# A two-layer decoder step: the indexer of layer 0 in one sequence, selection by tile, layer 1's attention steps in another order

## The reference, cut to what matters

```
I[t,s] = sum_h w[t,h] * relu(q_idx[t,h] . k_idx[s]) * 64**-0.5      # 8 heads, 64 wide, one shared key
keep[t] = top 128 (prompt) or 256 (sample) causal keys of I[t]      # ties: lowest index first
A[t]    = softmax over keep[t] of q.k * 64**-0.5, times V           # mixer A; mixer B (stick-breaking) uses all keys
C[t]    = (softmax1 - lambda * softmax2) V                          # layer 1, 8 heads, 4 KV heads
```

## Time and profile before

| | |
|---|---|
| median of 3 runs | 2282.15 us (2279.0 to 2286.1) |
| profiled execution | 2285.52 us, span 2283.7 us |
| busy | TensorE 2009.0, VectorE 742.9, ScalarE 420.9, GpSimd 267.4 us |
| granted TensorE clock | 0.938 of full on average |
| read from HBM | 255.30 MB, 115 GB/s over the span |

### The profile page before, as it was taken

The page is one execution under the profiler, slowest core; times in us unless marked ns, Lnnn a source line. Parts: engine busy times, 40 slices in busy tenths (PEclk is TensorE's granted clock), DMA queues, the critical chain, the costliest instruction groups (busy, mean ns, idle before and its releaser), DMA issues.

```text
span 2283.7 us, 32506 instructions
## 1 busy us (share of the span) xinstructions
PE 2009.0 (88%) x11272; PEld 1443.8 (63%) x11272; DVE 742.9 (33%) x1642; ACT 420.9 (18%) x771; POOL 267.4 (12%) x482
## 2 busy tenths in 40 slices
PE   7889957887768999999998997777788999999996
PEld 5447624544556777777776772344466777777775
DVE  2268975646501421110001421655523311200002
ACT  1120114454502200000001200333333100000000
POOL 3000221221110000000000000232200000000000
PEclk9999977988779999999999998998899999999998
DMA  7101053967641122111211113888701221212111
GB/s 236 41 22 64 0 218 142 338 237 271 231 176 65 56 70 68 64 65 65 73 64 64 48 63 119 283 291 266 263 21 54 69 69 64 73 57 73 64 65 59
DMA packets 95091, 264.45 MB, mean 116 GB/s; under 512 B 13650, under 2 KB 20051, under 8 KB 94355
## 3 DMA queue, kind: packets, MB, share of 16 engines
q0 software_dynamic: 46560, 167.80, 20.9%
q1 hardware_dynamic: 44146, 88.86, 11.5%
q10 hardware_dynamic: 4288, 6.51, 0.8%
HBM read 255.30 MB, written 7.82 MB: 115 GB/s over the span
## 4 chain that ended last, share of the span: by engine, by line
PE 70%; DVE 16%; DVEq 3%; ACT 3%; issue 3%; ACTq 2%; DMA 2%; SPq 1%; PEldq 0%
PE ps L485 53%; DVE arena L1427 4%; PE ps L541 2%; PE ps L842 1%; DVE arena L1308 1%; DVE small L1684 1%; PE ps L907 1%; DMA arena<-in_kv_ab 1%; PE ps L730 1%; PE ps L862 1%; PE ps L706 1%; PE ps L666 1%; DVEq L1312 1%; ACT arena L1219 1%; ACTq L329 1%
## 5 line engine op out<-in xcount | busy, mean ns | idle before, releaser
L485 PE MATMUL ps<-hs,wring 128*128 128x288 f32 x3520 | 872.4, 411 | 24.9 <-ACT hs L993 16.4
L485 PEld LDWEIGHTS ps<-hs,wring 128*128 128x128 f32 x3520 | 675.0, 192 | 220.5 <-issue 20.1
L485 PE MATMUL ps<-arena,wring 128*128 128x288 f32 x2048 | 500.5, 408 | 5.7 <-DVE arena L1342 5.7
L485 PEld LDWEIGHTS ps<-arena,wring 128*128 128x128 f32 x2048 | 391.0, 191 | 115.3 <-issue 6.6
L414 POOL DMA_DIRECT2D wring<-in_weights x170 | 90.2, 530 | 1386.3 <-PE ps L485 1385.0
L1340 DVE TENSOR_TENSOR arena<-arena,norm 128x576 f32 x64 | 48.5, 758 | 371.6 <-ACT arena L1012 365.2
L1297 DVE TENSOR_TENSOR norm<-norm 128x576 f32<-128x576 f32 x24 | 18.2, 759 | 448.6 <-ACT norm L1003 448.6
L1012 ACT ACTIVATE arena<-ps 128x576 f32 (+1 forms) x76 | 49.5, 651 | 527.2 <-PE ps L485 527.2
L1003 ACT ACTIVATE norm<-ps 128x576 f32<-128x576 f32 x32 | 20.8, 651 | 631.7 <-PE ps L485 631.7
L344 POOL DMA_DIRECT2D arena<-in_kv_ab x128 | 68.7, 537 | 278.6 <-PE ps L716 155.7
L344 POOL DMA_DIRECT2D arena<-in_kv_c x128 | 68.7, 537 | 215.6 <-PE ps L907 95.6
(11 more groups left out here) (231 smaller groups left out, 1804.8 us busy)
## 6 DMA issues: line engine op xcount, KB each, us to landing
wring<-in_weights POOLq DMA_DIRECT2D x174, 512.0 KB, 3.7
arena<-in_kv_ab SPq DMA_DIRECT2D x128, 320.0 KB, 5.0
arena<-in_kv_ab POOLq DMA_DIRECT2D x128, 320.0 KB, 6.5
arena<-in_kv_c SPq DMA_DIRECT2D x128, 256.0 KB, 4.0
arena<-in_kv_c POOLq DMA_DIRECT2D x128, 256.0 KB, 4.6
arena<-in_w_v_ab SPq DMA_DIRECT2D x1, 2592.0 KB, 24.6
xs<-in_x_t SPq DMA_DIRECT2D x4, 576.0 KB, 9.3
out_y_t<-xs SPq DMA_DIRECT2D x4, 576.0 KB, 2.8
```

The costliest lines, as they stand in the source:

```text
L485: mm = pe.matmul(out[:, h * 512:h * 512 + TH], wring[:, slot, k], inp[:, b * KD + k, h * TH:(h + 1) * TH], start=(b == 0 and k == 0), stop ...
```

## The change: what it does

**Indexer.** The twelve prompt units and the eight sample batches run in one sequence, `ORDER_I`, on TensorE and ScalarE. All query blocks (`qz8`) and head weights (`wz`, 32 columns for each batch) are staged once ahead of it. The Relu results of all eight batches are kept (`relu8`). The weighted sums come at the end: pair `p` of batches goes to partitions 32p to 32p+31 of `ps[2]` and `ps[3]`, by matmuls with 32 columns of weights. `clear` is gone.

**Rotations of mixer A** move from between the token-major tiles to behind the last five of the 13 projections, into `ps[2]` and `ps[3]`.

**Selection by tile.** After the search only tile 0 (the samples) is turned into a mask ahead of the attention; tiles 1 to 3 are done by `chosen(t)` in steps 1, 2 and 3 of the attention, ahead of `q_max(t)`. A memset and the wait for the store of the indexer keys move ahead of the search.

**Layer 1's steps.** On TensorE `p_turn` goes to the head of the step, `p_sums` runs a step earlier than before (unit n-2), the five `c_turn` are spread as 0 | 1, 2 | 3 | 4 over the quarters, each ahead of its values. On ScalarE `p_turn_out` goes to the head. On VectorE `p_out` goes to the head (unit n-3), `c_out` and one `c_turn_out` ahead of `p_mix`.

The diff, cut to its core:

```diff
+        ROT_A = 8
+        s_i = norm0[:, 0:2048].rearrange("p (r x) -> p r x", r=2)
+        UNITS_I = [(2 * it + r, i) for it in range(2) for r in range(2) for i in range(1, 4)]
+        ORDER_I = "S0 P0 P1 S1 P2 S2 P3 P4 S3 P5 S4 P6 P7 S5 P8 S6 P9 P10 S7 P11".split()
@@ TensorE, indexer
+            def i_sample(b):
+                p, s = b // 2, b % 2
+                if s == 0:
+                    pe.wait_ge(kidx_landed[p], 16 * (PAGES if p < 2 else 2 * PAGES))
+                    if p < 2:
+                        pe.wait_ge(kidx_landed_pool[p], 16 * PAGES)
+                if b:
+                    pe.wait_ge(i_relu, b)
+                q = qz8[s][:, p]
+                for h in range(2):
+                    pe.matmul(ps[2][:, h * 512:(h + 1) * 512], q, kx[s][:, p * 1024 + h * 512:p * 1024 + (h + 1) * 512], start=True, stop=True)
+                pe.matmul(ps[3][:, 0:NS], q, qk[:, IK, SEQ:T], start=True, stop=True).then_inc(i_qk, 1)
...
+            pe.wait_ge(i_staged, 1)
+            for what in ORDER_I:
+                if what[0] == "P":
+                    i_prompt(int(what[1:]))
+                else:
+                    i_sample(int(what[1:]))
+            pe.wait_ge(i_relu, NB)
+            parts = [(ps[2], 0, 0, 512), (ps[2], 512, 512, 512), (ps[3], 0, HALF, NS)]
+            for n, (t, lo, at, w) in enumerate(parts):
                 for s in range(2):
+                    for p in range(NB // 2):
+                        mm = pe.matmul(t[32 * p:32 * p + 32, lo:lo + w], wz[:, 2 * p + s], relu8[2 * p + s][:, at:at + w],
+                                       start=(s == 0), stop=(s == 1))
@@ TensorE, rotations of mixer A behind the projections
+            dense(G_AB + N_I, O_AB + N_I, N_AB - N_I, hs, peel=N_AB - N_I, after=rotate_a)
+            pe.wait_ge(rope_read, 5)
+            token_major(0, wv, 640, 16)
@@ TensorE, layer 1
             for n in range(STEPS_C):
                 b, quarter = n // 4, n % 4
+                if 2 <= n < UNITS_C + 2:
+                    p_turn(n - 2)
                 if n < UNITS_C:
                     p_scores(n)
                 if quarter == 0 and b < NB:
                     c_keys(b, 0)
                     c_keys(b, 1)
+                if quarter == 0 and b:
+                    c_turn(b - 1, 0)
                 if quarter == 1 and b >= 2:
                     c_pick(b - 2)
+                if quarter == 1 and b:
+                    c_turn(b - 1, 1)
                 if quarter == 1 and b < NB:
                     for g in range(2, 5):
                         c_keys(b, g)
                 if quarter == 1 and b:
-                    c_turn(b - 1, 0)
+                    c_turn(b - 1, 2)
                 if quarter == 2 and b:
-                    c_turn(b - 1, 1)
+                    c_turn(b - 1, 3)
                     c_values(b - 1, 0)
-                    c_turn(b - 1, 2)
                     c_values(b - 1, 1)
                 if quarter == 3 and b:
-                    c_turn(b - 1, 3)
+                    c_turn(b - 1, 4)
                     c_values(b - 1, 2)
-                    c_turn(b - 1, 4)
                     c_values(b - 1, 3)
                     c_values(b - 1, 4)
                 if 2 <= n < UNITS_C + 2:
-                    p_turn(n - 2)
-                if 3 <= n < UNITS_C + 3:
-                    p_sums(n - 3)
+                    p_sums(n - 2)
@@ VectorE, selection
+            dve.wait_ge(ik_stored, 16)
+            dve.memset(qz0, 0.0)
...
+            def chosen(j):
+
+                w = SEL_W[j]
+                thr = thr_b[:, j:j + 1]
+                dve.tensor_scalar(out_p[:, 0:w], scores[j], thr, None, ALU.is_gt, ALU.add, accum_out=cnt[:, j:j + 1])
+                dve.tensor_scalar(eq_p[:, 0:w], scores[j], thr, None, ALU.is_equal, ALU.add, accum_out=cnt[:, 0:1])
+                dve.drain()
+                dve.tensor_tensor(rest[:, j:j + 1], C["topk"][:, j:j + 1], cnt[:, j:j + 1], ALU.subtract)
+                dve.tensor_tensor_scan(cum_p[:, 0:w], eq_p[:, 0:w], eq_p[:, 0:w], 0.0, ALU.add, ALU.bypass)
+                dve.drain()
+                dve.scalar_tensor_tensor(eq_p[:, 0:w], cum_p[:, 0:w], rest[:, j:j + 1], eq_p[:, 0:w], ALU.is_le, ALU.mult)
+                dve.drain()
+                dve.tensor_tensor(eq_p[:, 0:w], eq_p[:, 0:w], out_p[:, 0:w], ALU.add)
+                dve.drain()
+                dve.tensor_scalar(scores[j], eq_p[:, 0:w], -1.0, BIG, ALU.add, ALU.mult)
+                dve.drain()
@@ VectorE, layer 0's attention
+                if 1 <= t < 4:
+                    chosen(t)
                 if t < UNITS_A:
                     q_max(t)
@@ VectorE, layer 1
+                if 3 <= n < UNITS_C + 3:
+                    p_out(n - 3)
                 if n < UNITS_C:
                     p_max(n)
+                if quarter == 1 and b >= 2:
+                    c_out(b - 2)
+                if quarter and b:
+                    c_turn_out(b - 1, (1, 3, 4)[quarter - 1])
                 if 1 <= n < UNITS_C + 1:
                     p_mix(n - 1)
...
-                if 4 <= n < UNITS_C + 4:
-                    p_out(n - 4)
```

More of the change, by code:

```diff
@@ L530, in rotate, with token_major @@
                 return rot
-            def token_major(v0, w, width, landed_n, after=None):
+            def token_major(v0, w, width, landed_n):
                 pe.wait_ge(wv_landed, landed_n)
@@ L626, in rotate_a @@
+            pe.wait_ge(PH["I"]["read"], len(UNITS_I))
+            def rotate_a(j, jstat, static):
+                c = j - ROT_A
+                if c < 0:
+                    return
+                if c == 0:
+                    pe.wait_ge(pen_ready, 1)
+                pe.wait_ge(dense_out, N_I + c + 1)
+                if c >= 2:
+                    pe.wait_ge(rope_read, c - 1)
                 for h in range(2):
-                    mm = pe.matmul(ps[j % 2][:, h * 512:h * 512 + TH], C["rot"], qk[:, AQ + j, h * TH:(h + 1) * TH],
+                    mm = pe.matmul(ps[2 + c % 2][:, h * 512:h * 512 + TH], C["rot"], qk[:, AQ + c, h * TH:(h + 1) * TH],
@@ L1056, in _ @@
             act.activation(two(iw_t), halves(ps[3])[0:8], ACT.Copy, scale=8 ** -0.5).then_inc(iw_b, 1)
-            with act.Fori(0, NB // 2) as p:
-                for s in range(2):
-                    act.wait_ge(i_qk, p * 2 + (s + 1))
-                    act.wait_ge(i_add, p * 2 + (s + 1))
-                    act.activation(relu_s[:, s, 0:HALF], ps[2][:], ACT.Relu, scale=SCALE)
-                    act.activation(relu_s[:, s, HALF:IW], ps[3][:, 0:NS], ACT.Relu, scale=SCALE).then_inc(i_relu, 1)
-            prompt_indexer(s_i)
+            for what in ORDER_I:
+                if what[0] == "P":
+                    i_prompt(int(what[1:]))
+                else:
+                    i_sample(int(what[1:]))
             act.wait_ge(rope_done, N_I)
@@ L1070, in _ @@
                 act.activation(two(qk[:, j]), halves(ps[(O_AB + j) % 2]), ACT.Copy, scale=SCALE if query else 1.0).then_inc(dense_out, 1)
+                c = j - N_I - ROT_A
+                if c >= 0:
+                    act.wait_ge(rot_done, N_I + c + 1)
+                    if c == 0:
+                        act.wait_ge(PH["I"]["soft"], len(UNITS_I))
+                    if c >= 2:
+                        act.wait_ge(rope_done, N_I + c - 1)
+                    act.activation(two(sqs[:, c % 2]), halves(ps[2 + c % 2]), ACT.Copy).then_inc(rope_read, 1)
             for t in range(5):
@@ L1389, in _ @@
             dve.memset(pen_p, 0.0)
-            dve.memset(qz_i, 0.0)
+            for s in range(2):
+                dve.memset(qz8[s], 0.0)
+            dve.memset(wz, 0.0)
             dve.drain()
@@ L1420, in _, with count @@
+            dve.drain()
+            dve.sem_inc(i_staged, 1)
+            for k in range(len(UNITS_I)):
+                i_prompt(k)
+            dve.wait_ge(i_add, NB // 2)
+            dve.tensor_copy(pen_s[:, 0:HALF], ps[2][:])
+            dve.tensor_tensor(pen_s[:, HALF:IW], ps[3][:, 0:NS], C["mask_i"], ALU.add)
+            dve.drain()
+            dve.sem_inc(pen_ready, 1)
             scores = [pen_s] + [pen_p[:, OFF[i]:OFF[i] + (i + 1) * P] for i in range(1, 4)]
             swap = [i ^ 8 for i in range(32)]
-            def count(src, scalar, op, out=junk):
-                for j in range(4):
+            def count(src, scalar, op, out=junk, tiles=4):
+                for j in range(tiles):
```

213 lines of the change are left out of this document (73 added, 140 removed).

## The result

The changed kernel took 2197.52 us (median of 4 runs, 2190.5 to 2203.82) beside 2281.93 us for the kernel before: a ratio of 0.9628, with a 95% interval of 0.9592 to 0.9664. Timed again in a later experiment (after_again) it took 2200.1 us (5 runs) beside 2280.51, ratio 0.9645 (0.9624 to 0.9666). So it is 80 to 84 us faster. Forecast: 2206, range 2188 to 2236.

A forecast was written before the change was run, and what follows sets the result against it. VectorE's search and mask and a latency loop in layer 1 were taken as bounds, with TensorE and VectorE alternating in the indexer. Terms -28 - 12 + 4 - 40 = -76 gave 2209.5, or 2206 by the median; range 2188 to 2236.

The forecast's parts named there:

- Part 1: Indexer in one sequence: the search starts at 123.2 us instead of 151.8, 28 earlier, bounds 17 and 31.
- 29 for the sequence: Indexer: sample passes of 2.13 us each, 11.0 for prompt units and 1 of restart waits left, 29 us.
- three modes in the earlier trace: TensorE's tiling: L701, L706, L716 overlap by 0.07 us or more, so 14 mode changes add nothing visible.
- Part 2: Selection by tile: 12 us leave the 24.6 ahead of layer 0's attention; tiles 1 to 3 add 4 inside it.
- Part 3: New order of layer 1's steps: the DMA becomes the bound, 184 us against 224, -40, bounds -50 and -20.
- at 345 GB/s 171 us: Layer 1's attention: its 59.1 MB of transfers at 345 GB/s take 171 us.
- the 24 to 25: Sign of being right: layer 1's batches 24 to 25 us apart, with DMA share at 0.95.
- The allowance for gaps: Layer 1: 4 us while first batches go by TensorE and slots wait, 5 to 9 after the last landing.
- at 374 without gaps: Layer 1's favourable bound: transfers at 374 GB/s with no gaps give -50 us.
- Rival (b): Layer 1: key loads become a wait in each batch, batches stay near 28 us, kernel 2231; chance 0.11.
- rival (c): Layer 0's attention: tiles 1 to 3 fully on the path (+13), first loads late (+5), 2220; chance 0.06.
- (d): Layer 1: two slot turn-arounds per batch stand open, 42.6 us a batch, kernel slower at 2348; chance 0.02.

The follow-up runs named there:

- same_group: Changed kernel with the two loops of the indexer's weighted sums exchanged, the two products of a column group directly behind each other: 2190.86 us, a single time.
- l1_only: Kernel before with only the new order of layer 1's three step loops: 2237.79 us, ratio 0.9815.
- chosen_twice: Changed kernel with all passes of `chosen` but the scaling done twice for tiles 1 to 3: 2210.91 us, ratio 0.9692.
- half_pages: Two of four pages loaded per slot of layer 1's ring: on the changed kernel 2174.75 us, on the kernel before 2274.98 us; output not the reference's.
- out_first: Kernel before with only VectorE's output copy in layer 1 moved to the head of the step: 2268.47 us, ratio 0.9936.
- chosen_ahead: Changed kernel with tiles 1 to 3 chosen ahead of the attention's first step instead of inside its steps: 2211.74 us, ratio 0.9688.
- act_old: Changed kernel with ScalarE's layer 1 loop in the old order, TensorE's and VectorE's in the new one: 2226.36 us, ratio 0.9765.

## Why the prediction was right, point by point

Events in us, means over the traces in which the code up to that event is the same (4 of the old indexer, 9 of the new; for the stretch to the attention and for the attention 4 and 8; for layer 1 2 and 7):

| step | before | after | measured | forecast |
|---|---|---|---|---|
| first count of the search | 152.3 | 124.5 | -27.8 | -28 |
| from there to the attention | 171.2 | 160.7 | -10.4 | -12 |
| layer 0's attention | 345.7 | 347.7 | +2.0 | +4 |
| layer 1 | 256.35 | 206.9 | -49.4 | -40 |
| sum | | | -86 | -76 |

**Part 1, right, a missing clock term made up by smaller ones.** The terms: 29 for the sequence was 30.0 (86.91 to 116.93). The half clock at its start cost 2.8 of it (6.17 us from the first pass to the second, where the same round takes 3.35 at 96.56), which the sum did not have; the prompt units were cheaper, 9.9 for twelve (1.35 a pair, 1.13 alone) and not 11.0, and the records overlap a little at each change. The sums took 3.86 for 4.3, the copy and add 1.4 for 1.7. The choice between side by side and one after the other was settled by the nearest row, and same_group bears it out: about a quarter of the single-file time. The prediction reads three modes in the earlier trace rows, but L706 and L716 are both 128*32, so that row has one change of mode. The new sequence has fifteen between full and 64-row tiles, and apart from 0.26 us for ScalarE's Relu none shows a gap: the record of 0.33 us from 94.91 ends 0.07 us after the next shape's starts at 95.17, the same overlap as between prompt units of one shape. By the rule of the Trainium skill (TensorEngine Tiling (Array Packing), Key Properties) that tiles operate independently, the trace agrees with the four groups; the drain that it names for each change of mode is not visible here.

**Part 2, right in kind.** The stretch behind the search went from 24.6 to 12.5 us, the 12 forecast, but the search itself became 1 to 2 us longer (148.2 for 147.1), with VectorE busy 132.9 for 131.3 in 488 instructions for 489. GpSimd was busy 25.6 us in it and not 21.4, since the rotations moved there. The trace shows VectorE's small instructions drawn out beside them:

```profile
210.03 1.40 POOL L437 TENSOR_TENSOR arena<-arena,cst 128x576 f32<-128x576 f32 x1 [4.42 <-ACT norm L1078]
210.07 1.38 DVE L1437 COPY_PREDICATED isel<-arena,isel 128x4 int32<-128x4 int32 x1
211.39 1.41 POOL L438 TENSOR_TENSOR norm<-norm,cst 128x576 f32<-128x576 f32 x1
211.53 1.28 DVE L1439 TENSOR_TENSOR isel<-isel 128x4 int32<-128x4 int32 x1
```

The same two take 0.17 and 0.16 us at 150.20 and 150.44. In this search seven such instructions took 0.7 to 1.4 us, each beside a rotation, 7.0 us more than their usual time together; before, it was four, with 4.4 us. In l1_only, whose layer 0 is the old one, less of GpSimd's work fell into the search (18.7 us for 21.4), three instructions were drawn out, and the search was 3.3 us shorter than before. So the 12 forecast for the tiles are right, and a price for moving the rotations into the search, 1.4 us, was missing. The tiles cost 2.0 us by the means (forecast 4), and chosen_twice shows that the slack ends there. The small waits for the first loads stayed small (0.94 and 1.31), as forecast.

**Part 3, right bound, term too small, and the loop read by one wait of several.** That the old order was a loop of waits and the new one ends at the DMA is shown by the two half_pages kernels. Which waits made the loop is read less well: the prediction follows VectorE's output copy, and moving that gave 14 of 49 us. The wait of `c_turn` cost TensorE more (26.1 us to 9.8), stayed in out_first and is gone in the new order; the prediction names its cure in half a sentence and gives it no price. How the other 35 us divide between `c_turn`, the earlier `p_turn` and `p_sums` and ScalarE's order that these need is open. The forecast did not depend on it, since the change moved all of them at once and the size came from the next floor. The step that was mis-sized is "at 345 GB/s 171 us": a full ring moved 362 to 383 GB/s in the batches above, so they came 22.6 us apart, between the 24 to 25 that the prediction gave as a sign of being right and the 21 that would show it wrong. Over five batches six traces have 22.3 to 22.8 us each and a seventh, chosen_ahead, 24.1. The 345 was taken beside the lower of two windows of 15 us (343 and 374), neither of which says what a ring that is full for 170 us moves; the higher one was nearer. The allowance for gaps, 4 and 5 to 9 us, was too large as well: the prediction's own stretch, 184 us by its sum, is 168.2 in the window above with the same bytes (351 GB/s times 168.2 us is 59.0 MB). At 370 GB/s they take 160, so 11 us of the miss are the rate and some 5 the gaps. In the means of the whole of layer 1 the term is 9 us larger than forecast, the value at its bound "at 374 without gaps". Rival (b), a new turn-around wait in each batch, did not come: TensorE's waits for pages were at most 2.8 us. Nor did rival (c), the tiles fully on the path, or (d). The whole forecast missed the medians by 4 to 8 us, this term alone by 9.

**What the medians gave.** 80 and 84 us against 86 in the traces and 76 forecast; the rest is within the scatter of layer 0's end (627.9 to 636.1 us in seven traces) and of the transfers.

## What to carry to other kernels

In a hand-ordered software pipeline, look for the operations at the end of an engine's step that another engine waits for at the start of its own: there can be more than one in series, on different engines, and moving one gives a fraction (14 of 49 us here). List them all in the waits, with their totals, before judging an order by one trial, and try the largest first: here it was not the one that the chain of a single step showed, and what it is worth by itself was not measured. Taking one move back out of a finished order (act_old) tells what the new order needs, and not what the old one lost by it. Once the loop is gone, size the gain by the next floor, and where short windows of a full resource differ (343 and 374 GB/s here), carry both rates through the sum. Work put into a stretch with slack can be nearly free up to a point and cost its full length beyond it; doubling it on the chip tells on which side of the point it is.

## What the runs showed of the hardware

**A full ring has no single rate.** Over five batches (third to seventh) seven of the eight traces with the new order and whole pages have 368 to 380 GB/s at DMA share 1.01 to 1.03, in batches of 22.3 to 23.0 us, and chosen_ahead has 351. The second trace of the changed kernel, and chosen_ahead over six batches:

```profile
1427.90:1542.37 114.47, 97.19 (x1275) 63.91 (x1266) 83.60 (x232) 52.34 (x138) 42.92 (x80) 1.00 1.01 368
```

```profile
1435.73:1580.19 144.46, 124.31 (x1507) 79.49 (x1507) 100.18 (x276) 62.89 (x165) 51.51 (x96) 0.94 0.98 350
```

The lower rate of chosen_ahead is in part no rate of a full ring. Its batches from 1436.8 to 1507.1 us moved 357 to 361 GB/s at share 1.00; the next took 26.0 us at share 0.91 and 313 GB/s. In it TensorE waited 2.86 us for pages, then ran a group of keys at half clock (3.64 us), and was busy 22.3 us at granted 0.87 where a batch takes 19. So a full ring gave 357 GB/s in some batches and 383 in others; what sets that stays open. The same kernel code for layer 1 took 204 to 212 us. The Trainium skill (DMA: Bandwidth & Descriptors, Specifications) has about 358 GB/s as what HBM gives one core; of the windows shown here 383, 369, 362 and, over five batches, 368 are over it and 350 is under, so that figure is not a ceiling for this kernel.

**VectorE's small instructions grow beside GpSimd's.** 0.16 us alone, 1.28 and 1.38 beside a rotation of 1.4 us, in the lines of part 2 above.

**Calls on different column groups overlapped in both orders tried.** 48 matmul records in 3.86 us with the groups in turn, 3.92 with the two calls of a group behind each other.
